# GLA sample states loaded beside the value rows, their products in four column groups, and head weights read two column tiles at a time

## The chip, the cores and the metric

The kernel runs on one core of one Trainium2 chip. The metric is device time in microseconds: the median of three runs. The core's engines are named as the profile names them: PE (TensorE matmul), PEld (its weight loads), DVE (VectorE), ACT (ScalarE), POOL (GpSimd) and SP (SyncE), which issues the weight transfers.

## What is computed

One step of a decoder layer, for 256 prompt tokens and 8 sample tokens that share all weights. One input projection feeds three token mixers (pooling, dilated attention, gated linear attention), whose outputs are gated and projected; cross-attention and a convolutional MLP follow. The change lies in the gated linear attention (GLA), which has four heads with keys of 256 and values of 512. For the sample every head carries a state of 256 x 512 for each of 8 sequences:

```
z = jnp.einsum('btd,dn->btn', h, w_in)
...
def gla_step(q, k, v, log_a, S):
    def step(S, xs):
        qt, kt, vt, at = xs
        S = jnp.exp(at)[..., None] * S + kt[..., None] * vt[..., None, :]
        return S, jnp.einsum('bhk,bhkv->bhv', qt, S)
```

## The kernel before

**Weights in slots.** All weights stream through a ring of three slots. A slot is 16 blocks of 128 x 128 (1 MB). SP loads it (`weights_raw`), ACT rounds it (`weights_hi`, L481), DVE makes the rest (`weights_lo`, L488), and PE multiplies: three matmuls per block, 48 per slot (L511 to L513), with 264 columns of tokens. The round of slot c+3 waits until slot c is projected. All engines run their programs in order and meet at semaphores; the order is written out by hand.

**A GLA head** (`gla_head`) is 12 slots: two tiles of queries, two of keys, four of values, four of the output gate. Each slot reads 128 columns of `w_in` over all 2048 rows and fills one of the PSUM banks 0, 1, 2 in turn. The bank is emptied right after its slot, by DVE for queries and keys (`gla_q`, `gla_k`), by ACT for values and gate. Between the slots stands the work of the prompt's chunks (transposes, scores, state update).

**The sample's tail of a head** (`gla_tail(k, h)`) is cut into steps k = 0 to 8. Step k of head h stands behind slot k of head h+1, and for the last head behind the slots of the gates. POOL loads states in twos (sequences 0 and 1, then 2 and 3, ...) into four buffers `gla_state_sample` (L768), and with each two their value rows spread over all partitions (`gla_v_spread`, L770), which come from a small scratch that POOL stores first (L752). ACT scales a state by its decay (L991), DVE adds key times value (L2031), PE takes the query product (L1497), and POOL stores the new state (L779). A buffer is loaded again only when its store has landed. `TAIL_SEQS` says which sequences step k handles on ACT and DVE: `[(0,), (1,), (2, 3), (4, 5), (6, 7)]`; PE takes them one step later, at k = 1 to 5. A state is 256 rows, so a sequence needs two fp32 matmuls (t = 0, 1), each of which appears as two records in the trace. All 16 of a head add up in the same 8 rows of bank 5. Then ACT copies the 8 rows (L995), and PE turns them (L1503).

**In POOL's program** the first four states of head h are issued at the start of `gla_tail(h)`, behind the store of the prompt's state, which waits for `S1_1`, the last update of head h (L753).

**Elsewhere in the same kernel** the dilated attention takes its sample products into four groups of output rows, 0, 32, 64 and 96 (L1623), each product 128 x 8 by 128 columns, and a slot that holds 1024 rows by 256 columns already exists for the branch weights (`pair_src`, L585).

Of the kernel before, what the change touches and what calls it, by code (L numbers as in the profile page):

```python
# [125 lines left out]
def build(nc, A):  # L126

    with ExitStack() as ctx:
# [79 lines left out]
        g_om = at("gla_o_sample_tokens", [NS, 512], yt2 + 4224)  # L208
# [133 lines left out]
        TAIL_SEQS = [(0,), (1,), (2, 3), (4, 5), (6, 7)]  # L342
# [3 lines left out]
        def steps(name, names):  # L346
# [4 lines left out]
        V_SET = steps("vector_setup", "sq1 var rstd sx1 par " + " ".join(f"lo{t}" for t in range(KB)) + " tz0 tz1 tz2 sb")  # L351
        P_SET = steps("tensor_setup", "par " + " ".join(f"x{t}" for t in range(KB)) + " tz0 tz1 tz2 sb")
        G_SET = steps("gpsimd_setup", "ident0 ident ones neg stat keep1 keep apart")
# [12 lines left out]
                     + " om os sq root yh0 yh1 yh2 yh3")  # L366
# [195 lines left out]
        def _(sp):  # L562
# [5 lines left out]
            with sp.Fori(0, 4) as h:  # L568
                for j in range(12):
                    kind, t = [("q", 0), ("q", 1), ("k", 0), ("k", 1)][j] if j < 4 else ("vr"[j // 8], j % 4)  # L570
                    col = {"q": h * 256 + COL_GQ, "k": h * 256 + COL_GK, "v": h * 512 + COL_GV,
                           "r": h * 512 + COL_GR}[kind]
                    load(sp, PH_GLA, j, h, w_cols(col + t * P))
# [143 lines left out]
        def _(pool):  # L717
# [15 lines left out]
            nc.gpsimd.memset(g_qm[:, :, :, :], 0.0).then_inc(G_SET("apart"), 1)  # L733

# [8 lines left out]
            def gla_head(h):  # L743
# [8 lines left out]
                pool.dma_start(d_vs[ds(h, 1)].rearrange("a b v -> (a b) v"), g_vs[:, :]).then_inc(vs_stored, 16)  # L752
                wait_loop(pool, V_GLA.at("S1_1", h))  # L753
# [19 lines left out]
            def gla_tail(h):  # L773
                for q in range(2):
                    ss_load(h, q)
# [94 lines left out]
        def _(act):  # L870
# [56 lines left out]
            act.wait_ge(*G_PRE.at("at0"))  # L927

# [5 lines left out]
            def gla_head(h, tail):  # L934
# [15 lines left out]
                for j in range(12):  # L950
                    act.wait_ge(projected, p.c(j, h) + 1)
                    if 4 <= j < 8:
                        nc.scalar.activation(g_vT[:, j - 4, :], bank[p.outs[j]][:, 0:T], ACT.Copy)\
                            .then_inc(evac[p.outs[j]], 1)
                    if j >= 8:
                        if j == 8:
                            act.wait_ge(*V_GT.at("osr", h - 1))
                        nc.scalar.activation(g_sr[:, j - 8, :], bank[p.outs[j]][:, 0:T], ACT.Silu)\
                            .then_inc(evac[p.outs[j]], 1)
# [25 lines left out]
            def gla_tail(k, h):  # L985
# [394 lines left out]
        def _(pe):  # L1380
# [108 lines left out]
            def gla_tail(k, h):  # L1489

                if 1 <= k < 6:
                    for b in TAIL_SEQS[k - 1]:
# [3 lines left out]
                        for t in range(2):  # L1496
                            mm = nc.tensor.matmul(bank[5][0:NS, :], g_qm[:, t, b, :], g_Ss[b % 4][:, t, :],  # L1497
                                                  start=b + t == 0, stop=b + t == NS)
                        mm.then_inc(P_GT(f"os{b}"), 1)
                if k == 6:  # L1500
                    pe.wait_ge(*A_GT.at("om", h))
# [13 lines left out]
            for t in range(8):  # L1515
                if t == 0:
                    pe.wait_ge(*V_SET.at("sb"))
# [391 lines left out]
        def _(dve):  # L1909
# [30 lines left out]
            nc.vector.tensor_copy(sbias_all[:, 0:SSEEN + 3], bank[6][0:8, 0:SSEEN + 3]).then_inc(V_SET("sb"), 1)  # L1940
            split_lo(dve, PH_GA, 0)
# [15 lines left out]
            def gla_head(h, tail):  # L1957
                p = PH_GLA
                for j in range(12):
                    ps = bank[p.outs[j]]  # L1960
# [3 lines left out]
                    if j < 2:  # L1964
# [645 lines left out]
```

## Time and profile before

| | us |
|---|---|
| median of three runs | 2808.69 (2805.4 to 2809.19) |
| the profiled execution | 2803.14 |
| its span in the trace | 2801.6 |
| PE busy in the span | 2673.8 (95%) |
| DVE busy | 1549.1 (55%) |
| ACT busy | 1223.3 (44%) |

The span is the time between the first and the last instruction that the hardware profiler saw. Busy is the time in which an engine ran at least one instruction. PE's matmuls overlap one another: one lasts about 0.28 us, but the next starts 0.12 us after it, so the pace is read from starts, not from durations. The four heads of the GLA lie between 55 and about 520 us of the span; the head loop (heads 1 to 3, with the tails of heads 0 to 2) takes 101 us for each head, and the tail of head 3 runs from 458 us.

### The profile page before, as it was taken

Reading aid. Unit: us, or ns where it says so; the run is one execution under the profiler, and the core shown is the slowest. Engines: PE = TensorE matmul, PEld = TensorE weight load, DVE = VectorE, ACT = ScalarE, POOL = GpSimd, SP = SyncE. Lnnn points to the kernel's source line nnn. Section 1 sums busy time; section 2 is a strip of 40 time slices with the busy share of each in tenths; the row PEclk is TensorE's granted clock in tenths of the full one; section 3 lists DMA queues with packets and bytes.
Section 4 is the critical chain, followed back from the end, with each engine's and each line's share of the span. In section 5 each row is a group of like instructions: output and inputs, shape, how many; then the busy total and the mean of one; then the engine's idle time right before and its main releaser. Section 6 shows DMA issues by size and latency. Waiting matters only on the chain. (4 is left out here: it accounts for less than half of the span.)

```text
span 2801.6 us, 53113 instructions
## 1 busy us (share of the span) xinstructions
PE 2673.8 (95%) x20951; PEld 2556.5 (91%) x20951; DVE 1549.1 (55%) x1937; ACT 1223.3 (44%) x1511; POOL 169.1 (6%) x270
## 2 busy tenths in 40 slices
PE   6799999999999999989999999998799999999997
PEld 5778878899999999979999889888799999999997
DVE  4455555444565555534654546442766665666666
ACT  4344444432444444434343534321555555444453
POOL 0020121000111111100000000120000000000000
PEclk9899999999999999989999999977899999999999
DMA  5686687766888888846666736753366666766564
GB/s 144 181 280 201 210 277 224 214 182 171 238 221 233 236 237 232 227 140 179 176 165 200 208 106 189 217 190 96 93 182 181 183 163 185 197 182 181 159 180 119
DMA packets 862672, 530.65 MB, mean 189 GB/s; under 512 B 13153, under 2 KB 842521, under 8 KB 861775
## 3 DMA queue, kind: packets, MB, share of 16 engines
q1 hardware_dynamic: 822583, 440.07, 57.5%
q0 software_dynamic: 23152, 74.95, 7.8%
q10 hardware_dynamic: 16832, 14.15, 1.6%
q8 instruction: 75, 1.23, 0.2%
q14 instruction: 30, 0.25, 0.0%
HBM read 499.79 MB, written 33.29 MB: 190 GB/s over the span
## 5 line engine op out<-in xcount | busy, mean ns | idle before, releaser
L511 PE MATMUL bank<-h_hi,weights_hi 128*128 128x264 f32 x4624 | 1333.4, 288 | 32.0 <-DVE weights_lo L488 14.4
L488 DVE TENSOR_TENSOR weights_lo<-weights_raw,weights_hi 128x2048 fp32r<-128x2048 f32 x407 | 932.1, 2291 | 771.3 <-ACT weights_hi L481 770.8
L512 PE MATMUL bank<-h_lo,weights_hi 128*128 128x264 f32 x4624 | 1316.1, 285 | 0.0
L513 PE MATMUL bank<-h_hi,weights_lo 128*128 128x264 f32 x4624 | 1314.5, 284 | 0.0
L511 PEld LDWEIGHTS bank<-h_hi,weights_hi 128*128 128x128 f32 x4624 | 877.2, 190 | 52.9 <-issue 29.6
L512 PEld LDWEIGHTS bank<-h_lo,weights_hi 128*128 128x128 f32 x4624 | 877.7, 190 | 2.0 <-issue 1.9
L513 PEld LDWEIGHTS bank<-h_hi,weights_lo 128*128 128x128 f32 x4624 | 872.9, 189 | 0.0
L481 ACT ACTIVATE weights_hi<-weights_raw 128x2048 fp32r<-128x2048 f32 x407 | 776.9, 1910 | 188.3 <-PE bank L513 186.2
L511 PE MATMUL bank<-y_hi,weights_hi 128*128 128x264 f32 x1232 | 352.9, 286 | 4.5 <-DVE y_lo L2280 3.8
L513 PE MATMUL bank<-y_hi,weights_lo 128*128 128x264 f32 x1232 | 351.7, 285 | 0.0
L512 PE MATMUL bank<-y_lo,weights_hi 128*128 128x264 f32 x1232 | 350.2, 284 | 0.0
L511 PEld LDWEIGHTS bank<-y_hi,weights_hi 128*128 128x128 f32 x1232 | 233.8, 190 | 5.1 <-DVE y_lo L2280 3.0
L513 PEld LDWEIGHTS bank<-y_hi,weights_lo 128*128 128x128 f32 x1232 | 233.9, 190 | 0.0
L512 PEld LDWEIGHTS bank<-y_lo,weights_hi 128*128 128x128 f32 x1232 | 233.9, 190 | 0.0
L1035 ACT ACTIVATE qkv<-bank 128x264 f32<-128x264 f32 x72 | 28.1, 390 | 257.3 <-PE bank L513 257.3
L511 PE MATMUL bank<-memory_normed_hi,weights_hi 128*128 128x256 f32 x256 | 73.9, 289 | 0.1
L512 PE MATMUL bank<-memory_normed_lo,weights_hi 128*128 128x256 f32 x256 | 72.7, 284 | 0.0
L513 PE MATMUL bank<-memory_normed_hi,weights_lo 128*128 128x256 f32 x256 | 72.5, 283 | 0.0
L1035 ACT ACTIVATE merged<-bank 128x264 f32 (+1 forms) x48 | 18.8, 392 | 105.8 <-PE bank L513 105.7
L1339 ACT ACTIVATE ffn_value<-bank,parameters 128x264 f32<-128x264 f32 x44 | 25.1, 571 | 90.0 <-PE bank L513 90.0
L1497 PE MATMUL bank<-gla_state_sample,gla_q_apart 128*8 128x512 f32 x128 | 58.2, 593 | 4.9 <-DVE gla_state_sample L2031 4.8
L1035 ACT ACTIVATE y_hi<-ffn_value 128x264 f32 (+1 forms) x44 | 18.7, 425 | 96.1 <-DVE ffn_value L2515 96.1
(353 smaller groups left out, 2251.9 us busy)
## 6 DMA issues: line engine op xcount, KB each, us to landing
weights_raw<-in_w_in SPq DMA_DIRECT2D x177, 1024.0 KB, 6.8
weights_raw<-in_w_up SPq DMA_DIRECT2D x88, 1024.0 KB, 5.8
weights_raw<-in_w_down SPq DMA_DIRECT2D x64, 704.0 KB, 4.8
gla_state_sample<-in_state_gla POOLq DMA_DIRECT2D x32, 512.0 KB, 6.1
out_gla_s<-gla_state_sample POOLq DMA_DIRECT2D x32, 512.0 KB, 6.3
weights_raw<-in_w_br_gla SPq DMA_DIRECT2D x16, 1024.0 KB, 6.0
weights_raw<-in_w_mix_out SPq DMA_DIRECT2D x16, 1024.0 KB, 6.1
weights_raw<-in_w_xkv SPq DMA_DIRECT2D x16, 1024.0 KB, 6.1
```

What stands on the lines that cost most here:

```text
L481: nc.scalar.activation(w_hi[:, r, :], raw[:, r, :], ACT.Copy).then_inc(hi_ready, 1)
L488: nc.vector.tensor_tensor(w_lo[:, r, :], raw[:, r, :], w_hi[:, r, :].bitcast(F32), ALU.subtract).then_inc(lo_ready, 1)
L511: nc.tensor.matmul(out, wh, xh, start=first and n == 0, stop=False)
L512: nc.tensor.matmul(out, wh, xl, start=False, stop=False)
L513: mm = nc.tensor.matmul(out, wl, xh, start=False, stop=last and n == len(blocks) - 1)
L1035: return nc.scalar.activation(out, in_, ACT.Copy)
L1339: nc.scalar.activation(c, bank[p.outs[j]][:, 0:T], ACT.Identity, scale=param(PC_CW + 176 + col, n), bias=param(PC_CB + col, n)).then_inc(S ...
L1497: mm = nc.tensor.matmul(bank[5][0:NS, :], g_qm[:, t, b, :], g_Ss[b % 4][:, t, :], start=b + t == 0, stop=b + t == NS)
```

## The change

Five things are altered.

1. **Loads of the head weights.** A slot is now 1024 rows by 256 columns: slot 2i holds the upper half of the rows of column tiles 2i and 2i+1, slot 2i+1 the lower half.
2. **Their products.** A slot gives 24 matmuls to one bank and 24 to the next; both banks are finished by the odd slot. So DVE takes queries 0 and 1 behind slot 1 and keys 2 and 3 behind slot 3, and ACT empties the values behind slots 5 and 7, the gate behind slots 9 and 11.
3. **Loads of the states.** POOL issues the first four states of head h right behind the store of its value rows, ahead of the wait for `S1_1`.
4. **Steps of the tail.** `TAIL_SEQS` is `[(0, 1), (2, 3), (), (4, 5), (6, 7)]`.
5. **Query products of the states.** They go to the rows 32 * (2 * (b % 2) + t): the four matmuls of two sequences lie in four column groups. ACT copies four strips of 8 rows, and the turning matmul adds them by `g_sel`, a sum over the four strips, which DVE makes once at the start.

```diff
-        TAIL_SEQS = [(0,), (1,), (2, 3), (4, 5), (6, 7)]
+        TAIL_SEQS = [(0, 1), (2, 3), (), (4, 5), (6, 7)]
...
                 for j in range(12):
-                    kind, t = [("q", 0), ("q", 1), ("k", 0), ("k", 1)][j] if j < 4 else ("vr"[j // 8], j % 4)
...
-                    load(sp, PH_GLA, j, h, w_cols(col + t * P))
+                    rows = slice(j % 2 * (D // 2), (j % 2 + 1) * (D // 2))
+                    load(sp, PH_GLA, j, h, [(0, KB // 2, 2 * P, w_in[rows, ds(pairs[j // 2], 2 * P)])])
...
                 pool.dma_start(d_vs[ds(h, 1)].rearrange("a b v -> (a b) v"), g_vs[:, :]).then_inc(vs_stored, 16)
+                for q in range(2):
+                    ss_load(h, q)
                 wait_loop(pool, V_GLA.at("S1_1", h))
...
-                    if 4 <= j < 8:
-                        nc.scalar.activation(g_vT[:, j - 4, :], bank[p.outs[j]][:, 0:T], ACT.Copy)\
-                            .then_inc(evac[p.outs[j]], 1)
+                    if j in (5, 7):
+                        for k in (j - 1, j):
+                            nc.scalar.activation(g_vT[:, k - 4, :], bank[p.outs[k]][:, 0:T], ACT.Copy)\
+                                .then_inc(evac[p.outs[k]], 1)
...
-                    nc.scalar.activation(g_om[:, :], bank[5][0:NS, :], ACT.Copy).then_inc(A_GT("om"), 1)
+                    for c in range(4):
+                        rows = slice(32 * c, 32 * c + NS)
+                        nc.scalar.activation(g_om[rows, :], bank[5][rows, :], ACT.Copy).then_inc(A_GT(f"om{c}"), 1)
...
-                    product(pe, p, j, j, h, H_BLOCKS).then_inc(projected, 1)
+                    for r in range(2):
+                        mm = product(pe, p, j, j - j % 2 + r, h, over(h_hi, h_lo, KB // 2, r * P, j % 2 * (KB // 2), 2 * P),
+                                     fresh=r == 0, first=j % 2 == 0, last=j % 2 == 1)
+                    mm.then_inc(projected, 1)
...
-                            mm = nc.tensor.matmul(bank[5][0:NS, :], g_qm[:, t, b, :], g_Ss[b % 4][:, t, :],
-                                                  start=b + t == 0, stop=b + t == NS)
+                            r = 32 * (2 * (b % 2) + t)
+                            mm = nc.tensor.matmul(bank[5][r:r + NS, :], g_qm[:, t, b, :], g_Ss[b % 4][:, t, :],
+                                                  start=b < 2, stop=b >= NS - 2)
...
-                                              ident[0:NS, 0:NS], start=True, stop=True)
+                                              g_sel[:, :], start=True, stop=True)
...
-                    if j == 0:
+                    if j == 1:
                         dve.wait_ge(*A_GLA.at("dec", h))
...
+                        for k in (0, 1):
+                            queries(k)
+                    if j == 3:
+                        for k in (2, 3):
+                            keys(k)
```

DVE in the head loop, from the loop's start to the second `weights_lo`. `gla_q` is the prompt's queries (it frees their bank), `gla_state_sample_94` and `_95` are the states of sequences 0 and 1. Before:

```order
L1965 TENSOR_SCALAR gla_q_sample<-bank 128x8
L1967 SCALAR_TENSOR_TENSOR gla_q<-bank,gla_q 128x256
...
L488 TENSOR_TENSOR weights_lo<-weights_raw,weights_hi 128x2048
...
L2031 SCALAR_TENSOR_TENSOR gla_state_sample_94<-gla_v_spread,gla_k_sample,gla_state_sample_94 128x512
...
L1965 TENSOR_SCALAR gla_q_sample<-bank 128x8
L1967 SCALAR_TENSOR_TENSOR gla_q<-bank,gla_q 128x256
...
L488 TENSOR_TENSOR weights_lo<-weights_raw,weights_hi 128x2048
```

And in the changed kernel:

```order
L489 TENSOR_TENSOR weights_lo<-weights_raw,weights_hi 128x2048
...
L2050 SCALAR_TENSOR_TENSOR gla_state_sample_94<-gla_v_spread,gla_k_sample,gla_state_sample_94 128x512
...
L2050 SCALAR_TENSOR_TENSOR gla_state_sample_95<-gla_v_spread,gla_k_sample,gla_state_sample_95 128x512
...
L1974 TENSOR_SCALAR gla_q_sample<-bank 128x8
L1976 SCALAR_TENSOR_TENSOR gla_q<-bank,gla_q 128x256
...
L1976 SCALAR_TENSOR_TENSOR gla_q<-bank,gla_q 128x256
...
L489 TENSOR_TENSOR weights_lo<-weights_raw,weights_hi 128x2048
```

The first query bank is now freed behind a whole `weights_lo` and four state updates (two for each sequence), where it was the first thing that DVE did.

PE in the head loop, behind slot 1. The matmuls of the first two sequences. Before, sequence 1 stands a whole slot later than sequence 0:

```order
L513 MATMUL bank<-h_hi,weights_lo 128x264
...
L1497 MATMUL bank<-gla_state_sample_94,gla_q_apart 8x512 x2
...
L511 MATMUL bank<-h_hi,weights_hi 128x264
...
L1497 MATMUL bank<-gla_state_sample_95,gla_q_apart 8x512 x2
...
L511 MATMUL bank<-h_hi,weights_hi 128x264
```

In the changed kernel:

```order
L514 MATMUL bank<-h_hi,weights_lo 128x264
...
L1507 MATMUL bank<-gla_state_sample_94,gla_q_apart 8x512 x2
L1502 REGISTER_ALU
L1507 MATMUL bank<-gla_state_sample_95,gla_q_apart 8x512 x2
...
L512 MATMUL bank<-h_hi,weights_hi 128x264
```

Both sequences now stand behind the same slot, and between them only the wait for the second sequence's update.

## Rows read from the trace of the kernel before

**Rows 1.** The page: PE's busy time; the group of the states' query products.

```profile
PE 2673.8 (95%) x20951; PEld 2556.5 (91%) x20951; DVE 1549.1 (55%) x1937; ACT 1223.3 (44%) x1511; POOL 169.1 (6%) x270
...
L1497 PE MATMUL bank<-gla_state_sample,gla_q_apart 128*8 128x512 f32 x128 | 58.2, 593 | 4.9 <-DVE gla_state_sample L2031 4.8
```

**Rows 2.** Busy by stretch: one head; its L1497 alone; products alone (after the heads).

```profile
155.00:256.00 101.00, 98.67 (x699) 83.25 (x699) 52.75 (x63) 48.10 (x64) 15.00 (x24) 1.00 0.76 235
...
155.00:256.00 101.00, 14.56 (x32) 2.46 (x32) 1.00 0.76 235
...
550.00:600.00 50.00, 50.00 (x415) 50.00 (x414) 21.39 (x14) 17.67 (x13) 0.00 (x0) 1.00 0.64 174
```

**Rows 3.** PE's waits up to 620 us: total, times, longest.

```profile
PE bank L511 <- DVE weights_lo L488: 14.4, 1, 14.4
...
PE bank L1497 <- DVE gla_state_sample L2031: 4.8, 5, 1.3
PE bank L1457 <- DVE gla_v_tokens L1999: 2.9, 3, 1.0
```

**Rows 4.** PE in order of time: start, length; two matmuls, then four, next slot.

```profile
167.86 1.88 PE L1497 MATMUL bank<-gla_state_sample,gla_q_apart 128*8 128x512 f32 x4 [1.27 <-DVE gla_state_sample L2031]
169.67 0.39 PE L511 MATMUL bank<-h_hi,weights_hi 128*128 128x264 f32 x1
...
183.49 3.60 PE L1497 MATMUL bank<-gla_state_sample,gla_q_apart 128*8 128x512 f32 x8
187.01 0.39 PE L511 MATMUL bank<-h_hi,weights_hi 128*128 128x264 f32 x1
```

**Rows 5.** PE in order of time: the dilated attention's products in four row groups.

```profile
779.09 1.61 PE L1623 MATMUL bank<-v_cache,probs_sample_apart 128*8 128x128 f32 x48
780.63 0.39 PE L511 MATMUL bank<-h_hi,weights_hi 128*128 128x264 f32 x1
```

**Rows 6.** ACT in order of time, at the start of the second head.

```profile
155.03 0.39 ACT L958 ACTIVATE gla_silu_r<-bank 128x264 f32<-128x264 f32 x1 [7.52 <-PE bank L513]
...
162.09 1.91 ACT L481 ACTIVATE weights_hi<-weights_raw 128x2048 fp32r<-128x2048 f32 x1
163.90 1.32 ACT L991 ACTIVATE gla_state_sample<-gla_state_sample,gla_log_decay 128x512 f32<-128x512 f32 x2
```

**Rows 7.** DVE in order of time, in the same head: updates of states.

```profile
166.32 1.41 DVE L2031 SCALAR_TENSOR_TENSOR gla_state_sample<-gla_v_spread,gla_k_sample,gla_state_sample 128x512 f32<-128x512 f32 x2
...
189.95 2.74 DVE L2031 SCALAR_TENSOR_TENSOR gla_state_sample<-gla_v_spread,gla_k_sample,gla_state_sample 128x512 f32<-128x512 f32 x4 [2.07 <-DMA gla_v_spread<-scratch_gla_v]
...
201.61 2.74 DVE L2031 SCALAR_TENSOR_TENSOR gla_state_sample<-gla_v_spread,gla_k_sample,gla_state_sample 128x512 f32<-128x512 f32 x4 [3.99 <-DMA gla_v_spread<-scratch_gla_v]
```

**Rows 8.** POOL in order of time, in the same head: stores and loads of states.

```profile
172.97 1.43 POOL L779 DMA_DIRECT2D out_gla_s<-gla_state_sample  x2 [16.62 <-DVE gla_state_sample L2031]
179.94 1.43 POOL L768 DMA_DIRECT2D gla_state_sample<-in_state_gla  x2 [5.54 <-DMA out_gla_s<-gla_state_sample]
...
183.52 1.43 POOL L779 DMA_DIRECT2D out_gla_s<-gla_state_sample  x2 [1.61 <-DVE gla_state_sample L2031]
193.42 1.43 POOL L768 DMA_DIRECT2D gla_state_sample<-in_state_gla  x2 [8.47 <-DMA out_gla_s<-gla_state_sample]
```

**Rows 9.** PE in order of time, at the end of its long wait in the first head.

```profile
89.59 0.59 PE L511 MATMUL bank<-h_hi,weights_hi 128*128 128x264 f32 x1 [14.36 <-DVE weights_lo L488]
```

**Rows 10.** DVE in order of time, at the same place.

```profile
87.24 2.29 DVE L488 TENSOR_TENSOR weights_lo<-weights_raw,weights_hi 128x2048 fp32r<-128x2048 f32 x1 [1.24 <-ACT weights_hi L481]
89.45 0.15 DVE L1965 TENSOR_SCALAR gla_q_sample<-bank 128x8 f32<-128x8 f32 x1
89.53 0.41 DVE L1967 SCALAR_TENSOR_TENSOR gla_q<-bank,gla_q 128x256 f32<-128x256 f32 x1
89.86 2.28 DVE L488 TENSOR_TENSOR weights_lo<-weights_raw,weights_hi 128x2048 fp32r<-128x2048 f32 x1
```

**Rows 11.** The page's DMA issues: KB each, median us from issue to landing.

```profile
weights_raw<-in_w_in SPq DMA_DIRECT2D x177, 1024.0 KB, 6.8
...
weights_raw<-in_w_br_dil SPq DMA_DIRECT2D x8, 1024.0 KB, 5.3
```

More of the change, by code:

```diff
@@ L350, in build @@
         A_SET = steps("scalar_setup", "sq0 sq2 root sx0 sx2 " + " ".join(f"hi{t}" for t in range(KB)))
-        V_SET = steps("vector_setup", "sq1 var rstd sx1 par " + " ".join(f"lo{t}" for t in range(KB)) + " tz0 tz1 tz2 sb")
+        V_SET = steps("vector_setup", "sq1 var rstd sx1 par " + " ".join(f"lo{t}" for t in range(KB)) + " tz0 tz1 tz2 sb sel")
         P_SET = steps("tensor_setup", "par " + " ".join(f"x{t}" for t in range(KB)) + " tz0 tz1 tz2 sb")
-        G_SET = steps("gpsimd_setup", "ident0 ident ones neg stat keep1 keep apart")
+        G_SET = steps("gpsimd_setup", "ident0 ident ones neg stat keep1 keep apart rows0")
         A_PRE = steps("scalar_gate", "abs exp ln ea")
@@ L733, in _ @@
             nc.gpsimd.memset(g_qm[:, :, :, :], 0.0).then_inc(G_SET("apart"), 1)
+            nc.gpsimd.memset(g_om[:, :], 0.0).then_inc(G_SET("rows0"), 1)
             pool.wait_ge(*V_SET.at("tz2"))
@@ L773, in gla_tail @@
             def gla_tail(h):
-                for q in range(2):
-                    ss_load(h, q)
                 for q in range(4):
@@ L1958, in gla_head, with queries @@
                 p = PH_GLA
+                def queries(k):
+                    ps = bank[p.outs[k]]
+                    nc.vector.tensor_scalar(g_qs[:, ds(h * 2 + k, 1), :], ps[:, None, NP:T], 1.0 / 16, None,
+                                            ALU.mult).then_inc(V_GLA(f"qs{k}"), 1)
+                    nc.vector.scalar_tensor_tensor(out=g_qt[:, k, :], in0=ps[:, 0:NP], scalar=1.0 / 16,
+                                                   in1=g_qt[:, k, :], op0=ALU.mult, op1=ALU.mult)\
+                        .then_inc(evac[p.outs[k]], 1)
@@ new lines, in keys @@
+                def keys(k):
+                    t, ps = k - 2, bank[p.outs[k]]
+                    k_in_chunks = ps[:, 0:NP].rearrange("p (m n c) -> p m n c", n=2, c=64)
+                    kh_in_chunks = g_kh[:, t, :].rearrange("p (m n c) -> p m n c", n=2, c=64)
+                    nc.vector.tensor_tensor(g_kx[:, t, :, :], k_in_chunks[:, :, 0, :], g_kx[:, t, :, :], ALU.mult)\
+                        .then_inc(V_GLA(f"kx{t}"), 1)
+                    nc.vector.tensor_tensor(kh_in_chunks[:, :, 1, :], k_in_chunks[:, :, 1, :],
+                                            kh_in_chunks[:, :, 1, :], ALU.mult).then_inc(V_GLA(f"ko{t}"), 1)
+                    dve.wait_ge(*V_GLA.at(f"kx{t}", h))
+                    for m in range(2):
+                        nc.vector.tensor_scalar(kh_in_chunks[:, m, 0, :], g_kx[:, t, m, :],
+                                                g_dec[:, t, 2 * m + 1:2 * m + 2], None, ALU.mult)\
+                            .then_inc(V_GLA(f"ke{t}_{m}"), 1)
+                    nc.vector.tensor_copy(g_ks[:, ds(h * 2 + t, 1), :], ps[:, None, NP:T]).then_inc(V_GLA(f"ks{t}"), 1)
+                    nc.vector.tensor_tensor(g_kt[:, t, :], ps[:, 0:NP], g_kt[:, t, :], ALU.mult)\
+                        .then_inc(evac[p.outs[k]], 1)
```

48 lines of the change are left out of this document (15 added, 33 removed).

## The prediction

> **What bounds the kernel now.** I read the page first: PE is busy for 2673.8 of 2801.6 us, no other engine for more than 55% [rows 1]. So a microsecond counts only if it is taken from PE's own stream or from one of its waits. Then the head loop by stretches: in the 101 us of a head PE is busy for 98.67 us, of which 14.56 us are the query products of the states [rows 2]. A plain slot is 48 matmuls at 50 us / 415, or 5.8 us [rows 2], and 12 slots make 69.6 us of the 101. Then PE's waits [rows 3]: 14.4 us once in the first head, 4.8 us for state updates (1.27 us in each of three heads, 1.0 us in the last tail), and 2.9 us for the value tokens (0.97 us in each of three heads). No wait of PE names a weight transfer, and the transfers' channel is busy for 0.76 of the head [rows 2].
>
> **The change part by part.** I set times inside one head, with slot 0 starting at 154.8 us, just ahead of ACT's row at 155.03 [rows 6].
>
> *Query products.* Four matmuls (eight records) in the same eight rows take 187.01 - 183.49 = 3.52 us from the first start to the next slot's start, two take 1.81 us [rows 4]. A head before has three such fours and two such twos: 3 x 3.52 + 2 x 1.81 = 14.2 us, and each of the five stretches also costs the slot behind it about 0.05 us of start-up. For the new form at 512 columns there is no row. The nearest is L1623, the same 8 output rows in four row groups but 128 columns: 48 records in 780.63 - 779.09 = 1.54 us, or 0.032 us each, and with 8 records at a quarter of the columns [rows 5]. The serial form gives 3.52 / 8 = 0.44 us a record at 512 columns, so 0.11 us at 128 if it goes by columns; the four groups are therefore 3.4 times as fast. Bounds for four matmuls: 3.52 / 4 = 0.88 us (four groups wholly side by side) and 3.52 us (one after the other). I take 0.88 us and 0.1 us for entry and exit, 1.0 us, since L1623 has the same form.
>
> *Can PE have both sequences at once?* The second half of each four waits for its own update, and that is DVE's. **Pair 0, 1:** ACT rounds the weights of slot 0's turn at 162.09 before; an added silu (0.3 us) moves it to 162.4, it ends at 164.3, and four scalings at 1.32 / 2 = 0.65 us [rows 6] are done at 166.9. DVE's remainder of the weights (2.2 us) ends at 166.6, the updates at 1.41 / 2 = 0.7 us each [rows 7] end at 168.0 and 169.4. PE ends slot 1 at 154.8 + 11.6 = 166.4, and can finish the four matmuls at 169.4 + 0.1 + 0.9 = 170.5: 4.1 us instead of 1.0. The earlier state loads don't shorten this; ACT's exponentials for the new head do not move. **Pair 2, 3:** DVE still has queries 0 and 1 (0.9 us), a remainder (2.2) and four updates (2.7) [rows 7, 10]: ready at 175.3, while slot 2 ends at 176.3. No wait, 1.0 us. The queries' bank is free at 169.9, and slot 2 needs it for its second half at 173.4, so that wait is covered by 3.5 us. **Pair 4, 5:** the first store is issued at 169.5 and lands 179.94 - 172.97 = 7.0 us later [rows 8]; the next states and value rows are usable 189.95 - 179.94 = 10.0 us after that [rows 7, 8], at 186.5. DVE is behind: two tiles of keys (2.2 us) and a remainder end 4.4 us behind slot 3, at 187.5, its updates at 188.9 and 190.2. Slot 4 ends at 188.9, the products at 191.5: 2.6 us. **Pair 6, 7:** the second store goes out at 178.5 and lands 193.42 - 183.52 = 9.9 us later, or, if it queues behind the loads ahead of it, 3.5 us after these (193.42 - 189.95), at 190.0; the states follow 201.61 - 193.42 = 8.2 us later, at 196.6 to 198.2; updates end 2.7 us on. Slot 5 ends at 197.7 (0.4 us of transposes stand ahead of it). So 2.6 to 4.3 us; I take 3.4.
>
> Sum for a head: 4.1 + 1.0 + 2.6 + 3.4 = 11.1 us, against 14.2 + 1.27 of wait + 0.2 of start-up (one stretch less, and the second half of the 0.1 us above) = 15.7 us. It gives 4.6 us.
>
> *The value tokens' wait.* PE waits 0.97 us in each head since ACT's first silu (slot 8) waits for the tail's DVE work and holds back the weights' rounding behind it. The silu now stands behind slot 9, so slot 8's rounding goes ahead at once and DVE copies the tokens 2 us earlier. I take the 0.97 us as gained: 5.6 us a head, 16.7 us for three.
>
> *The last tail* runs beside the gates, where ACT has no exponentials: the first pair costs 2.8 us, the others as above, 2.8 + 1.0 + 2.6 + 3.3 = 9.7 us against 14.2 + 1.0 + 0.2 = 15.4. It gives 5.7 us.
>
> *The first head's start* loses. PE's long wait ended at 89.59, when the fourth slot's remainder was there [rows 9]. It could run slots 0, 1 and 2 before. Now slot 2's second half needs the bank of queries 0, which DVE frees only behind that remainder (ends at 89.45) and 0.4 us of its own, as at 89.53 [rows 10]. So PE goes on at 90.0 with 24 matmuls more to do: 2.9 us + 0.4 us, and about 0.15 us for the added reduction that PE's first gate products wait for. 3.5 us. The bounds are 2.9 and 6 us (half a slot at half the clock).
>
> *At nothing:* the 256-column loads. The same 1 MB lands in 5.3 instead of 6.8 us where rows of that width are read [rows 11], but no wait of PE hangs on a load [rows 3]; it is room for the transfers of the states. The three added strip copies on ACT (0.5 us each) end some 4 us ahead of the turning matmul, behind slot 6. The turning matmul has 128 rows in place of 8, and its time goes by columns. The memset and the reduction are at the start. ACT's and DVE's doubled emptying costs DVE 1.1 us behind slot 3, counted above.
>
> **Total:** 16.7 + 5.7 - 3.5 = 18.9 us. The profiled execution has 2803.14, so 2784.2; from the median of the runs, 2808.69, it is 2789.8 us.
>
> *A rule against it.* L1623's rows show 48 weight loads and 48 matmuls in 1.54 us, so the loads lie beside the matmuls of other column groups [rows 5]. The Trainium skill, "TensorE: Matmul & The Clock Gate", Part 3 (packing small matmuls), says that a weight load overlaps matmuls in flight only when its row group differs; here all four share the rows. The trace speaks against it for column groups.
>
> **The rivals.**
>
> *All waits go (0.12).* If DVE's order lets all pairs be ready, a head costs 4.0 us instead of 15.7 and gives 12.7 with the tokens, the last tail 11.4: 38.0 + 11.4 - 3.5 = 45.9, or 2763 us. For it: the first states of a head are loaded two slots earlier. Against: pair 0, 1 hangs on ACT's row at 162.09, not on a load. Half of it gives 2776.
>
> *Weight loads don't hide (0.05).* Eight loads of 2.46 / 32 = 0.077 us [rows 2] per pair, 0.6 us x 16 pairs = 10 us: 2800 us. This is what the rule above would make of it. Only the 0.032 us per record speaks against it.
>
> *The groups don't overlap at 512 columns (0.10).* Each pair takes 3.5 us and the waits at its start stay: 5.2 + 3.5 + 3.6 + 4.5 = 16.8 against 15.7 + 0.97, nothing gained, and the start's 3.5 us are lost: 2812 us, within the noise. For it: no row shows four fp32 streams of 512 columns at once.
>
> *The moved state loads delay the weights (0.06), slower.* The first 3 MB of a head (four states and two spread rows) now start beside slots 9 and 10, not 11 and 0. A slot's load is issued when its predecessor's remainder is done, 4.4 us behind a slot's end, lands 6.8 us later [rows 11] and is rounded 17.4 us behind that end: 6.2 us of cover, and 7.2 us more between the remainder and its use. It decides once a load comes over 13.4 us late; 3 MB at 235 GB/s, the head's mean [rows 2], are 13 us, at most in turns with the weights. If each of four heads loses 7 us more than that, it is 2790 + 28 = 2818 us. Against it: before, the same transfers met other slots and cost PE nothing [rows 3].
>
> **How the numbers follow.** The forecast has 0.67. Its own range is 2778 to 2800: pair 6, 7 by 0.9 us a head either way, the pairs' 1.0 us up to 1.5 us (8 us in all), the start by 2 us, the tokens' wait by 3 us. With the rivals at 2776 and 2800 the range for 8 in 10 is 2774 to 2801. A measurement can tell about 0.2%, 5.6 us, from no change. Faster than 2803: forecast, full gain and unhidden loads, 0.84. Same: the groups that don't overlap, 0.10. Slower: 0.06.
>
> **What would show it.** Right: the products' busy time near 1.1 to 2.5 us a pair instead of 3.6, with records in fours a few ns apart; PE waiting for DVE's updates in the first, third and fourth pair, 6 to 8 us a head; no wait for the value tokens; a head of 95 us instead of 101; PE's long wait in the first head beginning 2.9 us earlier and ending on `gla_q`, 90.0 us. Wrong: records of a pair 0.43 us apart (no overlap); a wait of PE on `weights_lo` inside the heads (late loads); waits on banks in slot 2 or 4 (DVE too far behind); a head under 92 us (the updates come sooner than I think).

## The result, and the profile after

| | before | after |
|---|---|---|
| median, us | 2805.4 (2803.71 to 2809.19, five runs) | 2792.45 (2786.81 to 2794.65, five runs) |
| the profiled execution, us | 2803.14 | 2789.23 |
| its span, us | 2801.6 | 2787.7 |

The ratio is 0.9948, with a 95% interval of 0.9934 to 0.9962: 14.6 us faster (10.7 to 18.5), where 18.9 us were predicted. The predicted median was 2789.8 us, worked out from a median before of 2808.69 us over three runs; over five runs that median is 2805.4, so part of how near 2792.45 comes to it is luck, and the gains (14.6 and 18.9 us) are what to compare. It is easiest to read where the gain arose at four places of the two traces:

| | before, us | after, us | difference | predicted |
|---|---|---|---|---|
| the head loop starts | 154.83 | 157.17 | +2.3 | +3.5 |
| first slot of the gates starts | 457.18 | 445.09 | -12.1 (three heads: -14.4) | three heads: -16.7 |
| eleventh `gate` activation starts (end of the GLA) | 546.33 | 530.86 | -15.5 (last tail: -3.4) | last tail: -5.7 |
| end of the span | 2801.6 | 2787.7 | -13.9 | -18.9 |

The eleventh activation is the one behind the twelfth slot of the gates' stage; the texts recorded for the last two runs call it the twelfth.

**The page and the stretches** of the kernel after. First PE's busy time on the page, then two stretches with the busy time of each engine, the granted clock, the DMA share and GB/s, then (last two lines) the same stretches for the query products (now L1507) alone. They answer [rows 1, 2].

```profile
PE 2645.8 (95%) x20951; PEld 2547.8 (91%) x20951; DVE 1547.8 (56%) x1938; ACT 1229.6 (44%) x1523; POOL 169.7 (6%) x271
```

```profile
160.00:256.50 96.50, 91.78 (x695) 81.20 (x695) 52.16 (x63) 49.41 (x66) 15.27 (x23) 0.98 0.73 245
256.50:351.00 94.50, 90.63 (x698) 81.19 (x697) 52.23 (x63) 49.87 (x67) 15.28 (x23) 1.00 0.74 250
...
160.00:256.50 96.50, 8.38 (x32) 0.74 (x32) 0.98 0.73 245
256.50:351.00 94.50, 7.23 (x32) 0.74 (x32) 1.00 0.74 250
```

PE's busy time fell by 28 us, but the span only by 13.9: the products shrank from 14.56 us a head to 7.2 to 8.4, and half of what they gave came back as waits. The first of the two heads has a mean granted clock of 0.98, the second of 1.00; of that below.

**PE's waits** up to 620 us, as in [rows 3]: total, times, longest.

```profile
PE bank L512 <- DVE gla_q L1976: 17.6, 1, 17.6
PE bank L1507 <- DVE gla_state_sample L2050: 16.7, 21, 2.7
```

The long wait of the first head ends on the queries' bank, as predicted. The wait for state updates went from 4.8 to 16.7 us. The row for the value tokens (2.9 us before) is gone, and between 100 and 620 us the updates are all that PE waits for.

**A pair without a wait**, in PE's order of time, to be laid beside [rows 4].

```profile
178.69 1.04 PE L1507 MATMUL bank<-gla_state_sample,gla_q_apart 128*8 128x512 f32 x8
179.67 0.39 PE L512 MATMUL bank<-h_hi,weights_hi 128*128 128x264 f32 x1
```

Eight records take 179.67 - 178.69 = 0.98 us instead of 3.52: the four column groups run side by side at 512 columns. 1.0 us had been predicted.

### The profile page after: what moved, and what is told of

The parts are those of the page before. It is cut to its first block and busy times, and to the rows that moved or that the text cites. A ratio compares the mean times of both kernels' runs of the same rounds, so it can differ in the third digit from the quotient of the medians.

```text
span 2787.7 us, 53122 instructions
## 1 busy us (share of the span) xinstructions
PE 2645.8 (95%) x20951; PEld 2547.8 (91%) x20951; DVE 1547.8 (56%) x1938; ACT 1229.6 (44%) x1523; POOL 169.7 (6%) x271
## 5 line engine op out<-in xcount | busy, mean ns | idle before, releaser
L512 PE MATMUL bank<-h_hi,weights_hi 128*128 128x264 f32 x4624 | 1333.1, 288 | 34.7 <-DVE gla_q L1976 17.6
L1041 ACT ACTIVATE merged<-bank 128x264 f32 (+1 forms) x48 | 18.8, 392 | 106.9 <-PE bank L514 106.8
L2050 DVE SCALAR_TENSOR_TENSOR gla_state_sample<-gla_v_spread,gla_k_sample,gla_state_sample 128x512 f32<-128x512 f32 x64 | 43.8, 748 | 20.5 <-ACT gla_state_sample L995 10.8
```

The costliest lines, as they stand in the source:

```text
L512: nc.tensor.matmul(out, wh, xh, start=first and n == 0, stop=False)
L1041: return nc.scalar.activation(out, in_, ACT.Copy)
L2050: nc.vector.scalar_tensor_tensor(out=st, in0=g_vb[:, b % 4, :], scalar=g_ks[:, ds(h * 2 + t, 1), b], in1=st, op0=ALU.mult, op1=ALU.add).th ...
```

## Where the fourth pair's time goes

The prediction gave a head's four pairs 4.1 + 1.0 + 2.6 + 3.4 us. Measured in the first head of the loop: 1.63 us of wait and 2.20 (3.8), 0.97, 0.23 and 2.29 (2.5), and 2.58 and 3.14 (5.7). Only the last is off. Its chain, in order of time on each engine, with the idle time before a row and what ended it in brackets: POOL,

```profile
178.53 1.42 POOL L771 DMA_DIRECT2D gla_state_sample<-in_state_gla  x2 [4.63 <-DMA out_gla_s<-gla_state_sample]
179.95 0.57 POOL L773 DMA_DIRECT2D gla_v_spread<-scratch_gla_v  x1
180.59 1.43 POOL L780 DMA_DIRECT2D out_gla_s<-gla_state_sample  x2
191.65 1.43 POOL L771 DMA_DIRECT2D gla_state_sample<-in_state_gla  x2 [9.63 <-issue]
```

then ACT, DVE and PE,

```profile
199.40 2.56 ACT L995 ACTIVATE gla_state_sample<-gla_state_sample,gla_log_decay 128x512 f32<-128x512 f32 x4 [5.86 <-DMA gla_state_sample<-in_state_gla]
```

```profile
201.47 2.74 DVE L2050 SCALAR_TENSOR_TENSOR gla_state_sample<-gla_v_spread,gla_k_sample,gla_state_sample 128x512 f32<-128x512 f32 x4 [5.61 <-ACT gla_state_sample L995]
```

```profile
202.94 3.21 PE L1507 MATMUL bank<-gla_state_sample,gla_q_apart 128*8 128x512 f32 x8 [2.50 <-DVE gla_state_sample L2050]
206.08 1.47 PE L1442 MATMUL bank<-gla_q,gla_k 128*128 128x128 f32 x8
```

The store of states 2 and 3 is issued at 180.59, right behind 1.5 MB of loads for states 4 and 5, and lands 11.06 us later (9.5 to 11.0 us in the other three heads); loads, scalings and updates follow in a row. On top of that the eight records take 3.14 us where the third pair takes 2.29. Three stretches around it show PE's granted clock:

```profile
196.00:203.40 7.40, 4.90 (x40) 4.33 (x39) 1.93 (x3) 4.00 (x7) 0.00 (x0) 1.00 1.01 367
203.40:206.80 3.40, 3.40 (x11) 0.83 (x8) 3.40 (x4) 1.49 (x2) 1.43 (x2) 0.50 0.78 287
206.80:210.00 3.20, 3.20 (x30) 3.01 (x29) 0.21 (x1) 2.41 (x5) 0.40 (x1) 1.00 0.94 287
```

Behind a stretch in which PE worked for 4.9 of 7.4 us the clock was at 1.2 GHz for 3.4 us, over the pair and the first scores behind it. This happened in three of four heads (203.4, 394.5, 490.1 us), never in the kernel before between 100 and 600 us. In the head without it the pair is

```profile
298.62 1.03 PE L1507 MATMUL bank<-gla_state_sample,gla_q_apart 128*8 128x512 f32 x4 [1.35 <-DVE gla_state_sample L2050]
299.95 1.03 PE L1507 MATMUL bank<-gla_state_sample,gla_q_apart 128*8 128x512 f32 x4 [0.30 <-DVE gla_state_sample L2050]
```

and the head lasts 94.51 us, not 96.84. So there are two candidates for the 2.3 us that the fourth pair costs too much: the store's place in POOL's queue, and the clock.

## Experiments

"Gates" is the start of the eleventh gate activation against the kernel before (546.33 us); it holds the whole GLA and nothing behind it. The changed kernel has -15.5.

**One column group.** All four matmuls go to the same 8 rows again; the other three strips are filled with zeros, all else stays.

```diff
-                            r = 32 * (2 * (b % 2) + t)
-                            mm = nc.tensor.matmul(bank[5][r:r + NS, :], ...
+                            mm = nc.tensor.matmul(bank[5][0:NS, :], ...
```

> The changed kernel with part 5 undone on PE: all sixteen matmuls of a head add up in the rows 0 to 7 of bank 5 again (one column group); the four strip copies on ACT stay, three of them write zeros. If the four column groups run side by side and this is worth what it saves on PE: each pair takes 3.5 us from start to end instead of 1.0 (2.2 where the second update comes late), a head takes 101 to 102 us instead of 96.8, the program about 2789 + 20 = 2809 us. If the waits for DVE's updates hide most of it (rival), pairs 1, 3 and 4 end at almost the same time and a head loses only 3 us: about 2801 us. The clock stays at full level at the fourth pair.

Measured: 2803.19 us against 2804.51 for the kernel before, one run. Gates -2.0. The heads, from first pair to first pair, last 99.5, 99.5 and 98.2 us instead of 96.8, 94.5 and 95.3: 2.6 to 5 us more each, nearer to the rival (3 us) than to the theory (101 to 102 us a head). PE in order of time at the first and the second pair:

```profile
171.19 3.59 PE L1507 MATMUL bank<-gla_state_sample,gla_q_apart 128*8 128x512 f32 x8 [1.55 <-DVE gla_state_sample L2050]
180.72 3.60 PE L1507 MATMUL bank<-gla_state_sample,gla_q_apart 128*8 128x512 f32 x8
```

The fourth pair doesn't wait at all, and no clock falls. The groups take 2.55 us from each of 16 pairs, 41 us, and are worth 13.4 us (-15.5 against -2.0): two thirds come back, at the updates and at the clock.

**Groups alone.** The kernel before, with the column groups and nothing else of the change.

> The kernel before with part 5 alone: the products in four column groups, with the strip copies and the sum over strips; slots, loads and steps as before. If the products' time on PE is what counts (rival), each head gives 2 x 0.85 + 3 x 2.55 = 9.3 us and the program takes 2770 us. Theory: from the second pair on, the updates come when they come; in the kernel before they are ready at 182.8, 192.7 and 204.4 us against products that start at 183.5, 193.0 and 203.1, and the loads behind them wait for stores. Only the part up to the last update is gained: the last products end at about 205.3 instead of 206.6, so 1.3 us plus up to 2 us a head where the chain itself moves up: 2792 to 2800 us.

Measured: 2801.12 us, ratio 0.9978 (0.9961 to 0.9996); gates -2.6. PE's waits up to 620 us:

```profile
PE bank L1503 <- DVE gla_state_sample L2040: 26.8, 17, 5.2
...
PE bank L1462 <- DVE gla_v_tokens L2008: 2.9, 3, 1.0
```

What the matmuls give is waited away: 4.8 us became 26.8. The clock fell too, in four stretches (at 297.7, 400.1, 488.9 and 499.1 us) of 20.5 us in all, where the kernel before has none between 100 and 600 us. The rival (2770 us) is out; the theory's range (2792 to 2800 us) was missed by 1 us, with less gained than it said. By themselves the groups pay little.

**Old slots.** The loads and products of the head weights as before (parts 1 and 2 undone), parts 3 to 5 kept.

> The changed kernel with parts 1 and 2 undone: slots of 2048 rows by 128 columns, a bank emptied behind each slot, as before; column groups, state loads and steps of the tail stay. Theory: the wide slots cost time on PE (2.3 us at the first head's start, and two tiles of keys at once delay the third pair by about 1.3 us in each head) and give back the value tokens' wait (0.97 us in each of three heads): 2.3 + 1 = about 3 us faster than the changed kernel, 2786 us. Rival: the shorter transfers (1 KB rows) are what makes room for the states, and without them the fourth pair's states come later: 3 to 8 us slower than the changed kernel.

Measured: 2788.66 us, ratio 0.9945 (0.9923 to 0.9967), the same as the changed kernel; gates -16.7, 1.2 us better and not 3. Two waits of PE:

```profile
PE bank L512 <- DVE weights_lo L489: 15.2, 1, 15.2
...
PE bank L1462 <- DVE gla_v_tokens L2008: 2.9, 3, 1.0
```

Both price tags of the wide slots are there with opposite signs, 2.9 us for the value tokens and about as much at the start (the head loop starts 3.2 us earlier), and nearly cancel.

**Late loads.** The first four states of a head are loaded at the start of `gla_tail` again (part 3 undone).

> The changed kernel with part 3 undone: the first four states of a head are loaded behind the store of the prompt's state again. Theory: the first pair hangs on ACT's exponentials, not on the loads, but the loads now land (issued 1 us behind the store at 250.6, usable 10 us later at about 262) still before ACT's scaling at 263.5: nothing changes for states 0 and 1; the value rows of 2 and 3 land 2 us later, also in time. So within 1 us a head of the changed kernel: 96.8 to 97.8 us. Rival: the early loads are what lets both sequences of the first pair be ready, and without them each head loses 2 us or more.

Measured: 2788.32 us, one run; gates -14.8. It is no slower than the changed kernel by more than 0.7 us of gates, so the early loads are worth next to nothing. Only the last tail shows them, with one wait of 5.5 us for an update. There it costs 2.7 us; in the three heads ahead of it this run is 2.5 us faster. Old slots (-16.7, without parts 1 and 2), groups alone (-2.6, without parts 1 to 4) and this one together point to part 4, the regrouped steps, as what makes the column groups pay. That is an inference: part 4 was not run by itself.

**Stores first.** POOL stores states 2, 3 before it loads states 4, 5.

```diff
-                    if q < 2:
-                        ss_load(h, q + 2)
+                    if q == 1:
+                        ss_load(h, 2)
+                        ss_load(h, 3)
```

> The changed kernel with one change in POOL's program: the store of the states 2 and 3 is issued before the loads of 4 and 5, since its data is ready 1.2 us ahead of the landing that those loads wait for (177.3 against 178.5 us); nothing waits longer for it. Theory: the fourth pair is late because this store queues behind the loads of 4 and 5 and their value rows (issued at 180.6, landed at 191.7). Issued at 177.4 it lands at about 187 and the last states follow at 195 to 196, ahead of slot 5's end at 200.2: the fourth pair takes 1.0 to 2 us instead of 5.7, the drop of the clock there is gone, and a head takes 92.5 to 94 us; in all 10 to 16 us faster than the changed kernel, 2773 to 2779 us in its profile. Rival: the transfers are limited by bandwidth (the channel is full from 180 to 203 us), the last states come at the same time and nothing changes, or the third pair is delayed instead.

Measured: 2776.52 us, ratio 0.9893 (0.9877 to 0.991); gates -33.3, so 17.9 us more than the changed kernel, where 10 to 16 had been expected. Heads of 91.82 and 91.81 us. POOL in order of time, and PE's wait for updates:

```profile
177.97 1.42 POOL L780 DMA_DIRECT2D out_gla_s<-gla_state_sample  x2 [4.17 <-DVE gla_state_sample L2051]
179.45 1.42 POOL L771 DMA_DIRECT2D gla_state_sample<-in_state_gla  x2
...
184.98 1.42 POOL L771 DMA_DIRECT2D gla_state_sample<-in_state_gla  x2 [3.54 <-issue]
```

```profile
PE bank L1508 <- DVE gla_state_sample L2051: 7.7, 16, 1.6
```

The store goes out 2.6 us earlier and lands after 7.0 us (184.98 - 177.97; 6.4 to 7.1 over four heads), not 11.06. The last states are loaded 6.7 us earlier, the fourth pair takes 0.97 us without a wait, and the clock stays up. The queue's order was the first cause; with the gap that it made the falls of the clock are gone, too. How much of the 17.9 us needs the column groups is open: no kernel was run with stores first and one group.

**Fill.** In the changed kernel, 14 matmuls whose result nobody reads stand before the wait of the fourth pair, and keep PE busy in the gap.

> The changed kernel with 14 added matmuls of 128 x 128 by 264 columns on PE ahead of the fourth pair, into a bank that is free and read by nobody; they lie in the 2.2 to 2.8 us in which PE waits for the last updates. Theory: the granted clock falls to half for 3.4 us at the fourth pair in three of four heads since PE had little to do for some 5 us (the wait, then the four narrow products with another wait between); that stretches the pair from 2.29 to 3.14 us and the prompt's scores behind it from 0.98 to 1.40 us. With the added matmuls the clock stays at full level there, the pair takes 2.3 us and the scores 1.0 us, and the heads' end comes 3 to 4 us earlier (2784 us), although PE does more. Rival: the fall comes from something else (transfers, the other engines), and the pair still takes 3.14 us, with 1.7 us of matmuls added where the wait is shorter.

Measured: 2790.69 us, one run; gates -16.5. PE around the fourth pair:

```profile
201.54 1.86 PE L1505 MATMUL bank<-h_hi 128*128 128x264 f32 x14
204.09 1.03 PE L1512 MATMUL bank<-gla_state_sample,gla_q_apart 128*8 128x512 f32 x4 [0.69 <-DVE gla_state_sample L2055]
205.42 1.03 PE L1512 MATMUL bank<-gla_state_sample,gla_q_apart 128*8 128x512 f32 x4 [0.29 <-DVE gla_state_sample L2055]
```

All four fourth pairs take 2.29 us and no clock falls between 100 and 600 us: added work, and nobody is slower for it. From the first pair of the first tail to the eleventh gate activation it is 529.84 - 171.72 = 358.12 us, against 530.86 - 170.48 = 360.38: 2.3 us, where I had expected 3 to 4. Piece by piece, from first pair to first pair and at last to the gates:

| | first | second (no fall) | third | last tail |
|---|---|---|---|---|
| changed kernel, us | 96.84 | 94.51 | 95.29 | 73.74 |
| fill, us | 95.59 | 95.87 | 94.63 | 72.03 |

The three pieces with a fall are 3.6 us shorter together, the one without is 1.4 us longer, since its fourth pair comes 32.66 us behind the first and not 31.30. So a fall costs 1.2 us, as the pair (0.85 us) and the scores behind it (0.4 us) say, and the clock did give the 3 to 4 us; what is missing is a later landing in one head. Another 1.2 us was lost ahead of the first pair, 1.0 of it in the long wait of the first head, 18.6 us in this execution. Of the 2.3 us that the fourth pair costs too much in the first head, the clock is 0.85.

**Start.** In the first head DVE frees the queries' banks before it makes the next remainder of the weights.

```diff
+                    if isinstance(h, int) and j == 0:
+                        dve.wait_ge(projected, p.c(1, h) + 1)
-                    if j == 1:
+                    if j == (0 if isinstance(h, int) else 1):
                         dve.wait_ge(*A_GLA.at("dec", h))
```

> The changed kernel with one change in DVE's program in the first head only: queries 0 and 1 are taken, and their banks freed, ahead of the fourth slot's remainder and not behind it. Theory: PE's long wait ended at 89.1 on DVE's query, which stood behind a remainder of 2.2 us that itself waited for ACT (86.55 us). The query's inputs are there at 84.6, so PE goes on at 85.3 us, works off slot 2's second half at half clock by 90.6 and starts the fourth slot then and not at 94.5 us: everything behind it comes 3.5 to 4 us earlier. Rival: the fourth slot's remainder is the limit anyhow and PE gains nothing, or only the 0.9 us that the queries took in front of the second remainder.

Measured: 2790.03 us, one run; gates -18.8, 3.3 us better than the changed kernel (3.5 to 4 expected). PE's long wait in the first head, which was 17.6 us:

```profile
PE bank L512 <- DVE gla_q L1976: 13.7, 1, 13.7
```

**All of it.** Stores first, the new start, and in steps 0 and 3 the tail's work of ACT and DVE ahead of their work on the weights. The cut shows ACT; DVE's program is changed in the same way.

```diff
+                    if j in (0, 3):
+                        tail(j)
                     split_hi(act, p, j, h)
-                    tail(j)
+                    if j not in (0, 3):
+                        tail(j)
```

> The changed kernel with the stores first on POOL, the early queries in the first head, and in steps 0 and 3 the states' scaling and updates ahead of the weights' rounding and remainder on ACT and DVE. Theory: the first pair waits for DVE's updates (1.6 us, and 1.2 us between its halves) since these stand behind 4 us of weights' work on each engine that is not urgent; the third for the same reason (0.2 and 1.3 us). With the states first all four pairs take 1.0 us, a head takes 87 to 89.5 us instead of 91.8 (stores first alone), the start gives 4 us, and the heads' end lies 12 to 18 us ahead of the run with the stores first; the program takes 2750 to 2765 us. Rival: the weights' work is now late, and PE waits for it in slots 3 and 6, or the states of the third pair are not there yet and block ACT, so that a head takes as long as before the change.

Measured: 2768.92 us, ratio 0.986 (0.9833 to 0.9886), 39 us faster than before; gates -39.9, heads of 91.07 and 91.0 us. PE's waits:

```profile
PE bank L512 <- DVE gla_q L1980: 14.9, 1, 14.9
...
PE bank L1511 <- DVE gla_state_sample L2059: 4.8, 11, 1.0
```

The first pair no longer waits (1.09 us in all), the pairs of a head come to 1.09 + 2.13 + 3.36 + 0.98 = 7.6 us, against 3.8 + 0.97 + 2.5 + 0.97 = 8.3 with the stores first alone. The theory is missed: it had heads of 87 to 89.5 us and the heads' end 12 to 18 us ahead of stores first, and got 91.0 us and 6.6 us (39.9 - 33.3), half of it (3.3) the new start. What the first pair gained went mostly to the second, which now waits between its halves, and to the third, which waits 1 us for its updates. This kernel has the lowest median of all that were run.

**States first in step 1 too.**

> As the run with all three edits, but the states go first in step 1 too. There the second pair took 2.13 us (its second half waited for DVE) and the third waited 1.0 us, then 1.3 us between its halves, since the second store went out at 173.7 us and the loads of 4 and 5 behind it. Theory: the updates of 2 and 3 end 2.4 us earlier, and so do the store and the loads: the second pair takes 1.0 us, the third 1.0 to 1.5 us without a wait, and a head 87.5 to 89 us instead of 91.0; the heads' end comes 6 to 10 us earlier than in that run, the median is 2757 to 2764 us. Rival: the weights' remainder of slot 4 is now late and PE waits for it in slot 4, 1 to 2 us a head, or the last two pairs' transfers collide, and nothing is won.

Measured: 2771.47 us, ratio 0.9875 (0.9859 to 0.9892); gates -36.0. The second pair falls from 2.13 to 0.97 us, but the third waits 2.0 to 3.6 us instead of 1, and in one head the clock falls for 3.4 us again. The 6 to 10 us expected did not come: the gates are 3.9 us later than with all of it, and the intervals overlap.

**Old slots with all of it.** Stores first, and states first in steps 0, 1 and 3, on 128-column slots, where the start needs no mending.

> The same edits (column groups, early loads, stores first, states first in steps 0, 1 and 3) on slots of 2048 rows by 128 columns, with a bank emptied behind each slot as before. It asks what parts 1 and 2 are worth where nothing else holds PE back. Theory: the wide slots give back the value tokens' wait (0.97 us in each of three heads) and nothing else, so a head takes 1 us longer than with wide slots and the heads' end lies 2 to 4 us later. Rival: two tiles of keys at once behind slot 3 (1.1 us more on DVE ahead of the third pair's updates) cost as much as that, or the longer transfers (512 B rows) delay the states, so that it is either equal or more than 6 us later.

Measured: 2770.7 us, ratio 0.9876 (0.986 to 0.9893); gates -35.7. The theory had put the heads' end 2 to 4 us later than with wide slots, the rival at no difference. Three waits of PE:

```profile
PE bank L512 <- DVE weights_lo L489: 14.2, 1, 14.2
...
PE bank L1507 <- DVE gla_state_sample L2047: 5.9, 14, 1.3
PE bank L1466 <- DVE gla_v_tokens L2014: 2.9, 3, 1.0
```

The kernel with the same steps on wide slots has -36.0 by the gates and 0.9875: here, too, the two layouts of the slots can't be told apart.

**The same two kernels, profiled again.** In the first profiles of stores first and of all of it, the gates were 33 and 40 us earlier, but the ends of the span only 21 and 28 us (the text recorded for the run has 29.2 for the second; the spans, 2801.6 and 2773.8, give 27.8). The rest was lost at 1.8 to 1.9 ms, in the cross-attention.

> The same program as the kernel with stores first, states first and the new start, profiled once more. In its first profile the twelfth gate activation stood 39.9 us earlier than before, but the end only 29.2 us; the rest lay between 1770 and 1950 us, where the granted clock was at half for one stretch of 95.6 us, against 17.1 + 17.1 + 37.5 in the kernel before. Theory A (which stretches the chip takes at half clock in that stage differs from execution to execution, with the place at which the stage falls): the gain at the gates is again 39 to 41 us, and the half-clock total of the stage comes out other than 95.6 us, with the end 34 to 39 us earlier than before. Theory B (the earlier end of the GLA costs it by the program, transfers say): 95.6 us at half clock again, and the end 28 to 30 us earlier.

> The changed kernel, profiled once more. In its first profile the clock fell for 3.4 us at the fourth pair of heads 1, 3 and the last, not of the second; the twelfth gate activation stood 15.5 us earlier than before. Theory A (the falls belong to the gap in PE's work, and which of them are hit varies a little): the fourth pairs wait 2.4 to 2.9 us again, two to four of four take 3.1 us, and the gates stand 14.5 to 17 us earlier than before. Theory B (the falls were a chance of one execution): no half clock between 150 and 500 us, and the gates 18 us earlier.

Measured for all of it: gates -38.1, end of the span -35.2 (the first time -39.9 and -27.8). The stretch of 95.6 us from where the clock first falls, in the kernel before, in all of it, and in its second profile:

```profile
1852.90:1948.50 95.60, 86.25 (x430) 78.75 (x430) 22.59 (x94) 12.57 (x32) 7.51 (x10) 0.63 0.38 118
```

```profile
1811.05:1906.65 95.60, 85.57 (x331) 75.47 (x331) 19.38 (x88) 6.51 (x22) 7.52 (x10) 0.50 0.35 111
```

```profile
1811.90:1907.50 95.60, 85.86 (x386) 76.73 (x386) 19.97 (x91) 9.55 (x27) 7.52 (x10) 0.57 0.36 111
```

The mean granted clock was 0.63, 0.50 and 0.57, and PE got through 430, 331 and 386 records. One program gave two different numbers, so at least this much belongs to the execution and not to the program. For the changed kernel the gates were 15.7 us earlier; the fourth pairs waited 1.8 to 2.9 us, and the clock fell at two of the four, for 3.4 us at 202.4 and for 6.8 us at 393.6 us. Theory A in both, though the gates of all of it lie 1 us outside its range.

The runs without a trace say the same. If the loss belonged to the programs, the medians would fall short of the gates:

| | gates | median, from the ratio |
|---|---|---|
| changed kernel | -15.5, -15.7 | -14.6 |
| groups alone | -2.6 | -6.2 |
| old slots | -16.7 | -15.4 |
| stores first | -33.3 | -30.0 |
| all of it | -39.9, -38.1 | -39.3 |
| states first in step 1 too | -36.0 | -35.1 |
| old slots with all of it | -35.7 | -34.8 |

None does by more than its interval (some 4 to 7 us either way). The gain at the gates is the gain. Three of the four first profiles of the fastest kernels had the long stretch; why so many is open.

## Why the prediction was right, point by point

The forecast's mechanism held: groups side by side, waits for updates instead, the tokens' wait gone, a slower start. Its sum was 18.9 us, of which 15.5 arrived at the gates.

- **Query products, 1.0 us for four matmuls:** 0.98 us. The step from 128 to 512 columns held, and the rivals "the groups don't overlap" and "weight loads don't hide" fell with the same row.
- **Pairs one to three, 4.1 + 1.0 + 2.6:** 3.8 + 0.97 + 2.5. DVE as the engine that comes last was right. The sign of 6 to 8 us of waits a head did not show as such: the profile gives 16.7 us over four heads, since between the halves of a pair PE mostly counts as busy.
- **Pair 6, 7, 3.4 us:** 5.7 us in the first head, 3.7 and 5.4 in the next two. This is the term that was mis-sized. To lay the times beside the prediction's, which count from a slot 0 at 154.8 us, take off 2.4 us, since slot 0 started at 157.17. The second store then went out at 178.2 us (178.5 predicted) and landed at 189.3, between the two landings that the prediction had seen (188.4 and 190.0). But the updates began at 199.1 us, not at 196.6 to 198.2: from the loads' issue to the first scaling it was 199.40 - 191.65 = 7.8 us, where the kernel before had 199.73 - 193.42 = 6.3 us. Its row in ACT's order of time:

```profile
199.73 2.57 ACT L991 ACTIVATE gla_state_sample<-gla_state_sample,gla_log_decay 128x512 f32<-128x512 f32 x4 [4.43 <-DMA gla_state_sample<-in_state_gla]
```

  That is 1.7 us more than the middle that the 3.4 us stand for, and 0.85 us of half clock in the pair, with 0.4 us in the scores behind it, stood in no term. The prediction took the place of the store behind the loads as a given of the stage; it is an order in POOL's program, and turning it round was worth 17.9 us, more than the whole change.
- **A head, 5.6 us:** 4.8 on average, 14.4 for three. In the head without a fall of the clock it was 100.78 - 94.51 = 6.3, with pairs of 11.1 us as predicted: some 0.7 us more came from somewhere that I can't name. If it came in every head, it hid part of the fourth pair's loss in the average, and that is luck.
- **Value tokens, 0.97 us a head:** gone as predicted, and back with the old slots.
- **The last tail, 5.7 us:** 3.4, since its fourth pair took 2.77 us of wait and 3.14 us, as above.
- **The first head, 3.5 us lost:** 2.3. PE resumed at 89.31 and not 90.0, 0.3 us earlier than before and not 0.4 later. The 24 matmuls took 94.48 - 89.31 = 5.17 us at half clock, but the fourth slot behind them took 2.5 us less than before, so they cost 2.6 us and not 2.9. PE in order of time, and two stretches, up to the 24th matmul and the slot behind it:

```profile
89.31 0.59 PE L512 MATMUL bank<-h_hi,weights_hi 128*128 128x264 f32 x1 [17.60 <-DVE gla_q L1976]
```

```profile
89.10:94.48 5.38, 5.17 (x25) 5.18 (x26) 2.75 (x4) 0.00 (x0) 0.00 (x0) 0.53 0.94 309
94.48:100.30 5.82, 5.82 (x50) 5.82 (x49) 2.29 (x1) 1.92 (x1) 0.00 (x0) 1.00 0.49 157
```

In both kernels PE runs at 1.2 GHz right behind the long wait. Before, the fourth slot bore this and took 8.35 us (mean clock 0.67); now the 24 matmuls bear it and the fourth slot takes 5.82.

- **State loads ahead of the weights (slower):** nothing. No wait of PE names `weights_lo` between 100 and 620 us.
- **All waits go (0.12):** not in this kernel. Of the rival's 45.9 us the kernel with all edits reached 39.9 at the gates, by the order of the stores and of ACT's and DVE's work and not by earlier loads.

## What to carry to other kernels

When a matmul stage is packed, look at the next thing that is late before the packing is priced: here 41 us of matmuls gave 2.6 us alone and 13.4 us with the regrouped steps, and the whole kernel gained 33.3 us once two stores and two loads changed places in one queue. Try a store that frees a buffer ahead of loads that are issued with it. Where a gain is judged by one trace, take it at a landmark right behind the changed stage, and check it against the medians of several runs: the stages behind it differed by 9 us between two executions of the same kernel.

## What the runs showed of the hardware that I had not expected

- **Column groups at 512 columns of fp32** cost 0.98 us for four matmuls of 8 output rows, against 3.52 us in one group: 3.6 times as fast.
- **A gap of 2.2 to 2.9 us** that ended in the four-group products was followed by 3.4 us at 1.2 GHz (once 6.8) in five of six cases in the two profiles of the changed kernel, gaps of 1.4 and 1.8 us were not, nor were the four gaps in which 14 matmuls without use stood. The price of a fall was 1.2 us.
- **A store right behind 1.5 MB of loads** in POOL's queue landed after 9.5 to 11.1 us, and ahead of them after 6.4 to 7.1 us.
- **The cross-attention** runs some 72 us (before, 17.1 + 17.1 + 37.5) to 96 us at 1.2 GHz, around its 256 matmuls of one column (line, operation and shapes; busy time, mean ns of one; in all of it, its stretch of 95.6 us):

```profile
L1848 PE MATMUL bank<-x_probs_sample,mem_v_cache 128*128 128x1 f32 x226 | 48.4, 351 | 2.4 <-DMA mem_v_cache<-in_cache_mem_kv 2.4
```

PE counts as busy for 85.57 of the 95.6 us there, and still the clock is down. How much of it is spent so differs between two executions of one kernel. No kernel was run that changes this stage.
